# Attention's first two score tiles set inside the last input group, two gates through tanh: one edit of a tuned chain of mixers

## The reference

```python
h = rmsnorm(x, pre_g[l])
proj = jnp.einsum('bsd,de->bse', h, w_in[l])
u_a, v_a, g_a, q, k, v, g_b = jnp.split(proj, idx, axis=-1)
y_a = gmlp_group(u_a, v_a, ...) * jax.nn.silu(g_a)
y_b = gqa_axial_attention(q, k, v, ...) * jax.nn.silu(g_b)
x = x + rmsnorm(jnp.concatenate([y_a, y_b], axis=-1) @ w_out[l], post_g[l])
...
# attention: 8 query heads, 2 key/value heads, head size 64, no mask
sc = jnp.einsum('bqkgd,bskd->bkgqs', qblk, k) * scale
p = jax.nn.softmax(sc, axis=-1)
o = jnp.einsum('bkgqs,bskd->bqkgd', p, v)
```

## Time and profile before

| | |
|---|---|
| median of three runs | 2312.51 us (2309.94 to 2312.78) |
| the profiled execution | 2307.94 us |
| its span, first to last instruction | 2306.2 us |
| mean granted clock of TensorE | 0.999 of full speed |
| busy: TensorE, VectorE, ScalarE, GpSimd | 98%, 47%, 39%, 12% of the span |
| start of attention, first and second mixer | about 272 and 832 us |

### The profile page before, as it was taken

The page is one execution under the profiler, slowest core; times in us unless marked ns, Lnnn a source line. Parts: engine busy times, 40 slices in busy tenths (PEclk is TensorE's granted clock), DMA queues, the critical chain, the costliest instruction groups (busy, mean ns, idle before and its releaser), DMA issues.

```text
span 2306.2 us, 28550 instructions
## 1 busy us (share of the span) xinstructions
PE 2268.0 (98%) x11640; PEld 1919.1 (83%) x11640; DVE 1077.0 (47%) x1439; ACT 888.5 (39%) x1426; POOL 274.0 (12%) x276
## 2 busy tenths in 40 slices
PE   8999999999999999999999999998999999999998
PEld 7887799988888789998788898887888888888887
DVE  4313399954333259983624152325334344342343
ACT  5222477744322257772444141323212222222232
POOL 0097200000029600000013020000000000000000
PEclk9999999999999999999999999999999999999999
DMA  6111000033311000003311101322111121124232
GB/s 202 37 55 37 1 1 1 1 137 120 92 46 55 19 1 1 1 22 113 141 59 42 60 19 37 118 66 91 47 55 52 39 55 46 45 98 149 92 127 73
DMA packets 104210, 141.48 MB, mean 61 GB/s; under 512 B 11670, under 2 KB 65094, under 8 KB 104102
## 3 DMA queue, kind: packets, MB, share of 16 engines
q1 hardware_dynamic: 104102, 139.97, 18.4%
HBM read 123.18 MB, written 16.78 MB: 61 GB/s over the span
## 4 chain that ended last, share of the span: by engine, by line
PE 94%; DVE 3%; ACT 1%; issue 1%; DMA 0%; DVEq 0%; SPq 0%; ACTq 0%
PE ps L199 24%; PE ps L201 24%; PE ps L200 24%; PE ps L974 5%; PE ps L989 3%; PE ps L990 3%; PE ps L961 2%; PE ps L962 2%; PE ps L938 1%; PE ps L228 1%; PE ps L925 1%; PE ps L275 1%; PE ps L1953 1%; PE ps L675 1%; DVE hT_lo L290 1%
## 5 line engine op out<-in xcount | busy, mean ns | idle before, releaser
L199 PE MATMUL ps<-w_hi,hT_hi 128*128 128x512 f32 (+1 forms) x1760 | 678.5, 386 | 2.4 <-DVE hT_lo L238 1.4
L201 PE MATMUL ps<-w_hi,hT_lo 128*128 128x512 f32 (+1 forms) x1760 | 672.0, 382 | 0.0
L200 PE MATMUL ps<-w_lo,hT_hi 128*128 128x512 f32 (+1 forms) x1760 | 671.6, 382 | 0.0
L183 DVE TENSOR_TENSOR w_lo<-w_raw,w_hi 128x2048 fp32r<-128x2048 f32 x89 | 207.6, 2333 | 539.4 <-ACT w_hi L167 536.8
L199 PEld LDWEIGHTS ps<-w_hi,hT_hi 128*128 128x128 f32 x1760 | 331.2, 188 | 66.8 <-issue 2.1
L201 PEld LDWEIGHTS ps<-w_hi,hT_lo 128*128 128x128 f32 x1760 | 331.1, 188 | 64.7
L200 PEld LDWEIGHTS ps<-w_lo,hT_hi 128*128 128x128 f32 x1760 | 331.4, 188 | 62.5 <-issue 0.5
L167 ACT ACTIVATE w_hi<-w_raw 128x2048 fp32r<-128x2048 f32 x71 | 135.9, 1914 | 502.2 <-PE ps L201 502.2
L199 PE MATMUL ps<-hT_hi,w_hi 128*128 128x512 f32 x832 | 324.2, 390 | 5.0 <-DVE X L2523 2.7
L201 PE MATMUL ps<-hT_hi,w_lo 128*128 128x512 f32 x832 | 323.7, 389 | 0.0
L200 PE MATMUL ps<-hT_lo,w_hi 128*128 128x512 f32 x832 | 323.7, 389 | 0.0
(11 more groups left out here) (203 smaller groups left out, 2363.3 us busy)
## 6 DMA issues: line engine op xcount, KB each, us to landing
w_raw<-in_ffn_w_up SPq DMA_DIRECT2D x44, 512.0 KB, 5.0
w_raw<-in_ffn_w_down SPq DMA_DIRECT2D x22, 1024.0 KB, 4.9
w_raw<-in_w_in SPq DMA_DIRECT2D x21, 1024.0 KB, 5.1
x_mid<-X SPq DMA_DIRECT2D x24, 512.0 KB, 2.7
w_raw<-in_gla_w_in SPq DMA_DIRECT2D x12, 1024.0 KB, 5.1
X<-in_x SPq DMA_DIRECT2D x16, 512.0 KB, 7.1
w_raw<-in_w_out SPq DMA_DIRECT2D x8, 1024.0 KB, 6.7
X<-x_mid SPq DMA_DIRECT2D x16, 512.0 KB, 7.4
```

The lines of the kernel that those rows point to most:

```text
L183: engine.tensor_tensor(self.p.w_lo[:, slot, 0:size], self.p.w_raw[:, slot, 0:size], plane(self.p.w_hi[:, slot, 0:size]), ALU.subtract).the ...
L199: nc.tensor.matmul(out, a_hi, b_hi, start=first, stop=False)
L200: nc.tensor.matmul(out, a_hi, b_lo, start=False, stop=False)
L201: return nc.tensor.matmul(out, a_lo, b_hi, start=False, stop=last)
```

## The change

It is made in both mixers, since they share the code.

- **TensorE.** `scores` becomes a method. Tiles 0 and 1 of attention are issued inside the last input group, tile 0 ahead of the second half of token tile 6 and tile 1 ahead of that of token tile 7. Attention's own loop starts its scores at n = 2. `turn_head` for the heads turned inside attention also waits for the seventh gate, which leaves bank 6.
- **ScalarE.** Gates 0 to 5 stay Silu. Then come exponential 0, a tanh of gate tile 6 into a new tile `E` with half of the inverse norm as scale, exponential 1, and the tanh of gate tile 7. The values' high half moves from n = 1 to n = 2, behind exponential 2.
- **VectorE.** Once a mixer it halves the inverse norm of the last two tiles (`dve_halve`), ahead of the keys' low halves. `dve_gate` makes a gate of a tanh: a multiply-add in place on `E`, then the product with the PSUM bank into `G`, which frees the bank. It stands behind maximum 0 for gate 6 and behind maximum 3 for gate 7. The values' low half moves behind the low halves of the probabilities of step n = 2.

```diff
@@ MixerIn.pe
         for t in range(1, TT):
+            if t >= TT - EARLY:
+                att.scores(pe, t - (TT - EARLY))
             pe_wide_tile(prog, 1, t, t, w.slot(unit + 1)).then_inc(self.acc_ready, 1)
+
+    def act_gate(self, act, t):
+
+        n = t - (TT - EARLY)
+        act.wait_ge(self.acc_ready, len(MIXER_ORDER) * TT + t + 1)
+        act.wait_ge(self.half_inv, 1)
+        self.p.nc.scalar.activation(self.E[:, n, :], self.p.ps[:, t, :], ACT.Tanh, scale=self.norm.stat[:, 1, t:t + 1]
+                                    ).then_inc(self.e_done, 1)
+
+    def dve_halve(self, dve):
+
+        ts = slice(TT - EARLY, TT)
+        self.p.nc.vector.tensor_scalar(self.norm.stat[:, 1, ts], self.norm.stat[:, 2, ts], 0.5, 0.0, ALU.mult,
+                                       ALU.add).then_inc(self.half_inv, 1)
+
+    def dve_gate(self, dve, t):
+
+        nc, n = self.p.nc, t - (TT - EARLY)
+        e = self.E[:, n, :]
+        dve.wait_ge(self.e_done, n + 1)
+        half = self.norm.stat[:, 1, t:t + 1]
+        nc.vector.tensor_scalar(e, e, half, half, ALU.mult, ALU.add).then_inc(self.e_step, 1)
+        dve.wait_ge(self.e_step, n + 1)
+        dve.wait_ge(self.ga_used, t + 1)
+        nc.vector.tensor_tensor(self.G[:, t, :], self.p.ps[:, t, :], e, ALU.mult).then_inc(self.acc_free, 1)
@@ MixerIn.act
                 for t in range(TT):
-                    take(v // 2 - 1, t)
+                    if v < MIXER_PIECES - 1 or t < TT - EARLY:
+                        take(v // 2 - 1, t)
+                    else:
+                        att.exponential(act, t - (TT - EARLY))
+                        self.act_gate(act, t)
@@ Attention.turn_head
             pe.wait_ge(self.doubled, item - KV)
+            self.gates(pe, TT - 1)
@@ Attention.pe
         for n in range(NT + 6):
-            if n < NT:
-                scores(n)
+            if EARLY <= n < NT:
+                self.scores(pe, n)
@@ Attention.act
-            if n < NT:
-                act.wait_ge(self.max_done, n + 1)
...
-            if n == 1:
+            if EARLY <= n < NT:
+                self.exponential(act, n)
+            if n == 2:
                 for g in range(KV):
                     nc.scalar.activation(self.VS[:, g, :, 0:HD], QKV[:, :, 640 + g * HD:640 + (g + 1) * HD],
@@ Attention.dve_first
+        self.inp.dve_halve(dve)
         for i in range(2 * KV):
@@ Attention.dve
-            if n == 2:
-                for g in range(KV):
-                    dve.wait_ge(self.v_hi, g + 1)
...
+            if n == 0 or n == 3:
+                self.inp.dve_gate(dve, TT - 2 if n == 0 else TT - 1)
             if 2 <= n < NT + 2:
...
+            if n == 2:
+                for g in range(KV):
+                    dve.wait_ge(self.v_hi, g + 1)
```

More of the change, by code:

```diff
@@ L551, in start @@
     return inp, att, sems
+EARLY = 2
 class MixerIn:
@@ L579, in __init__ @@
         self.wsR = prog.at("wsR", [P, H_A, P], kb + 56)
+        self.E = prog.at("E", [P, EARLY, WIDE], kb + 88)
+        self.half_inv = prog.sem("half_inv")
+        self.e_done = prog.sem("e_done")
+        self.e_step = prog.sem("e_step")
         self.acc_ready = prog.sem("acc_ready")
@@ L944, in last_output, with scores @@
         self.turn_o(pe, self.NT // 2 - 1, self.NT + 5)
+    def scores(self, pe, n):
+        prog, nc = self.p, self.p.nc
+        head, t = n // TT, n % TT
+        if t == 0:
+            pe.wait_ge(self.lo_done, 2 * (KV + head) + 2)
+            pe.wait_ge(self.k_top, 2 * KV)
+        if n >= 2:
+            pe.wait_ge(self.exp_done, n - 1)
+        else:
+            self.gates(pe, 2 * n + 2)
+        for half in range(2):
+            keys = self.KT_st[:, head // (H_B // KV), half * 512:(half + 1) * 512]
+            out = prog.ps[:, 2 * (n % 2) + half, :]
+            nc.tensor.matmul(out, self.QT_hi[:, head % 2, t * P:(t + 1) * P], keys, start=True, stop=False)
+            mm = nc.tensor.matmul(out, self.QT_lo[:, head % 2, t * P:(t + 1) * P], keys, start=False, stop=True)
+        mm.then_inc(self.s_ready, 1)
     def pe(self, pe):
         prog, nc, NT = self.p, self.p.nc, self.NT
[L949 to L963, removed]
         def turn_p(m):
@@ L1035, in act_first, with exponential @@
         self.q_hi(act, 0, 1)
+    def exponential(self, act, n):
+        act.wait_ge(self.max_done, n + 1)
+        if n >= 3:
+            act.wait_ge(self.p_turned, 2 * n - 4)
+        self.p.nc.scalar.activation(self.PR[n % 3][:].rearrange("p (a b) -> p a b", a=2),
+                                    self.p.ps[:, 2 * (n % 2):2 * (n % 2) + 2, :], ACT.Exp,
+                                    bias=self.nmx[:, n:n + 1], accum_out=self.sm[:, n:n + 1]
+                                    ).then_inc(self.exp_done, 1)
     def act(self, act):
@@ L1123, in dve @@
                                         ALU.max, negate=True).then_inc(self.max_done, 1)
-            if n == 2:
-                for g in range(KV):
-                    dve.wait_ge(self.v_hi, g + 1)
-                    nc.vector.tensor_tensor(self.VS[:, g, :, HD:P], QKV[:, :, 640 + g * HD:640 + (g + 1) * HD],
-                                            plane(self.VS[:, g, :, 0:HD]), ALU.subtract).then_inc(self.v_lo, 1)
+            if n == 0 or n == 3:
+                self.inp.dve_gate(dve, TT - 2 if n == 0 else TT - 1)
             if 2 <= n < NT + 2:
@@ L1138, in dve @@
                 nc.vector.reciprocal(self.inv[:, m:m + 1], self.sm[:, m:m + 1]).then_inc(self.inv_done, 1)
+            if n == 2:
+                for g in range(KV):
+                    dve.wait_ge(self.v_hi, g + 1)
+                    nc.vector.tensor_tensor(self.VS[:, g, :, HD:P], QKV[:, :, 640 + g * HD:640 + (g + 1) * HD],
+                                            plane(self.VS[:, g, :, 0:HD]), ALU.subtract).then_inc(self.v_lo, 1)
             if NT <= n < NT + 4:
```

## The result

The changed kernel takes 2317.41 us (median of eight executions) where the kernel before takes 2309.97 us (eight). One of the changed kernel's executions, of 5927.63 us, was disturbed; without it the median is 2316.10, and the ratio, which leaves it out, is 1.0029, interval 1.0018 to 1.0039. So the change makes the kernel slower by 0.29%, more than the 0.2% that the prediction took for no difference. The time lies inside the range (2309.5 to 2319.0), but the likeliest case, 2313.9 and "no difference", did not come. A second series with the same file gave 2316.9 against 2312.75, 1.0023 (1.0014 to 1.0032).

The account below looks back on a forecast made before the run. TensorE bounds the kernel except at attention's start, where waits cost 8.0 us. VectorE's chain makes the third turn 0.7 us later per mixer, 1.4 in all, added to the 2312.5 median: 2313.9 us, range 2309.5 to 2319.0.

Parts of the forecast that it names:

- the likeliest case: Attention start, clock holding: third turn 0.7 us later per mixer, 1.4 in all, 2313.9 us; chance 0.55.
- three gaps become one: TensorE at attention's start: three waits per mixer become one of about 4.5 us before the third turn.
- The order of the chain: Tanh, VectorE gates, maxima, exponentials, values' halves and low halves in sequence, putting the third turn at 283.78.
- a gate on VectorE: Gates 6 and 7: multiply-add 0.75, hand-over 0.15, product 0.61, together 1.51 us each.
- the forecast's +1.4: Third turn inside attention moves from 283.09 to 283.78, 0.7 us later per mixer, for both mixers together.
- The stated lower bound, +1.0: Least total delay of the third turns, with multiply-add 0.68 and hand-over 0.10; upper end +2.8.
- The estimate by the Trainium skill: VectorE gates: fp32 multiply-add in SBUF 0.42 us, each gate 1.18, in all +0.1.
- a fall in one or both mixers: TensorE's clock drops behind the long gap in attention; chance 0.33, of which 0.17 over 4.6 us slower.
- The price of a fall: Attention at half clock: 0.9 us for each of two turn batches, 0.7 for eight matmuls: 2.5, at least 0.7.
- the rival with two falls: Clock falls behind the long gap in both mixers: 2318.9 us; one fall 2316.4; any fall has chance 0.33.
- Tables: ScalarE: Exp and Tanh need separate table loads, 1.28 us each, 3.5 a mixer, 2320.8 us; chance 0.04.
- Faster: Waits at attention's start vanish, 8.0 us come back, 2304.5 us, needing a chain 3.0 shorter; chance 0.06.

Follow-up runs that it names:

- experiment 6: Kernel before the change, with three useless reductions on VectorE behind the maximum of tile 3 in each mixer; 2321.14 us, ratio 1.0047.
- number 7: Changed kernel with values' halves on GpSimd, one-instruction gates on VectorE (GpSimd halves G), gate 7 at n = 2; 2306.8 us, ratio 0.998.
- number 4: Changed kernel with all eight gates by Silu on ScalarE before the exponentials, no tanh or gates on VectorE; 2321.21 us, ratio 1.0038.
- 8: Changed kernel with each VectorE gate made one instruction instead of two, GpSimd halving G later; 2313.5 us, ratio 1.0013.
- 3: Changed kernel with the second VectorE gate moved from n = 3 to n = 2; 2309.9 us, ratio 0.9998.
- 10: The same kernel as number 7, run again; 2305.79 us, ratio 0.9976.
- Experiment 1: Changed kernel with twelve useless 512-wide matmuls on TensorE in the long gap before the third turn; 2309.93 us, ratio 0.9994.

## Why the prediction was wrong in its likeliest case

**Right.** Within attention TensorE waits only at its start. The likeliest case had three gaps become one, for `PT_lo`, in front of the third turn: said about 4.5, is 4.06. The order of the chain was right, the table load is hidden, Exp and Tanh share a table, the gates end in time.

**The term that was mis-sized: a gate on VectorE.** The prediction took 1.51 us; it is 1.19. The multiply-add is 0.54 to 0.55 (said 0.75, after line 761), and the dependent product follows within 0.04 (said 0.15, after the earlier trace rows); the product was right at 0.60. Two gates, 0.65 us too much: the third turn, forecast for 283.78 in the time of before, is at 283.35 - 0.24 = 283.11. So the forecast's +1.4 for both mixers is 0.0. The stated lower bound, +1.0, failed as well, because the row it used as the least, 0.68, was not the least. The estimate by the Trainium skill ("VectorE: DVE Perf Modes", the perf-mode tier table) was 1.18 a gate, nearly the sum as measured, but by luck: its multiply-add of 0.42 is below the 0.55 that ran, and the 0.15 of hand-over from rows is above the 0.04. By it the forecast's chain was +0.1, against 0.0 as measured.

**The step that failed: the likeliest case had the clock hold.** The forecast without a fall had 0.55, a fall in one or both mixers 0.33. Two rows framed the gap, 7.99 us with a fall and 2.73 without, no row lay between, and holding got the larger chance without a reason from a row. All profiles with a gap of 4.06 to 4.28 (the changed kernel twice, experiment 6) fell in both mixers. Even the bound below was weaker than it looked: behind 2.76 at 1578.42 the clock fell in the changed kernel, and behind 2.53 and 2.10, with 0.95 shortly before, it fell in one mixer and held in the other. One row where the clock held was read as a limit, but it showed only that it can hold there. The Trainium skill ("TensorE: Matmul & The Clock Gate", "Why this matters for your kernels") warns of idle gaps between bursts of matmuls; the trace now agrees, and shows falls behind gaps as short as 1.90 us as well.

**The price of a fall** was put at 2.5 us, at least 0.7. It is 1.2 to 1.5 us where the clock is low for 3.4 us and 2.3 to 2.7 where it is low for 6.8. So 2.5 was right for the long kind, and the sum did not see that there are two. Two falls come to 3.5 in the one profile of the changed kernel and 4.8 in the other, not 5.0.

**What no case had:** falls in stages the change does not touch, 4.5 us of the profiled difference. Without them two falls come to 0.15% in the one profile and 0.21% in the other, about the bound of 0.2%; the falls elsewhere carry the time clearly over it. That the rival with two falls comes so near, +6.4 against +6.1 measured (2316.10 less 2309.97), is luck in part, from errors with opposite signs: the chain taken too long, the falls elsewhere left out. The likeliest case said +1.4; its 2313.9 looks nearer than that only because it starts from 2312.5, the median of three runs, where eight gave 2309.97.

**The rivals.** Tables: wrong, as held. Faster (2304.5, by a chain 3.0 us shorter): not by this change; number 7 comes near it. There the third turn is 14.07 behind the start of scores 0 (266.36 to 280.43), against 16.48 in the changed kernel: 2.4 us sooner a mixer. Its ratio of 0.9976 to 0.998 is 4.6 to 5.5 us of 2310, its granted clock that of before.

**What stays open.** Why the further falls, near 575, 1136, 1580 and 1597, come in one execution and not in another, behind gaps of 1.90 to 2.76 us that are the same in both. All five profiles with a fall in the second mixer (the changed kernel's two, 4, 6, 8) show one between 1136 and 1146 as well, but 3, 7 and 10, which held in the second mixer, have one near 1130, and only the changed kernel's two have those near 1580 and 1597. Whether a fall in attention makes the later ones likelier, or only another position of the same gaps, was not tried. Experiment 1 bears on it: with the gap filled the ratio goes from 1.0029 and 1.0023 to 0.9994, some 7 us, more than the 3.5 to 4.8 of the two falls in attention, which points to falls elsewhere becoming rarer too. Nor is it known from which gap on the fall is certain: 3.49 and more fell each time in these profiles, 2.1 to 2.5 in one mixer of two, and 3.3 (number 4) in both, in the second 0.56 us behind the gap's end. The smaller gaps shortly before the long one differ between these kernels too, and no run varies them alone.

## What to carry to other kernels

Several short waits of a stretch are not the same as one long wait of equal sum: look at the longest gap of TensorE that a change makes, and read the length of the first instructions behind it and the granted clock, before the busy shares. When a chain's engine is full, moving its producers earlier buys nothing until work leaves that engine; here values and half of a gate went to GpSimd, which was idle, and only then did early scores pay. Where a delay cannot be removed, matmuls of no use in the gap can keep the clock: here they cost nothing and took the ratio from 1.0023 to 0.9994.

## What the hardware showed unexpectedly

- Executions of one kernel differ in steps that go with the mean granted clock: the kernel before has spans of 2306.2 to 2306.7 (0.999), 2308.2 to 2309.8 (0.999 or 0.998) and 2310.8 to 2311.7 (0.997). That each step is one more fall is likely, but profiles show it only in part: experiment 1's, with one low stretch, spans 2308.1, and its executions at 0.999 span 2306.0 to 2306.3.
- A multiply-add in SBUF with two scalars per partition takes 0.54 to 0.55 us for 128x512 in fp32, less than the 0.68 at least of line 761, and the instruction that depends on it starts within 0.04.
- GpSimd makes two high parts of 128x512 in 1.18 us and two low parts in 2.53, about twice VectorE's 1.29 for the same two, where nothing waits for it.
- After a fall, the time until full clock differs: 286.14 in the first mixer, 2.8 us behind the start of the third turn; 849.33 in the second, 5.1 us behind it.
